# Paged decode attention in one core's kernel: cache pages transposed in 32 by 32 blocks on VectorE, scores in small tiles, pages gathered by GpSimd

## What is computed

```python
c_past = cache_ckv[page_table].reshape(b_s, past_len, KV_RANK)          # 8 x 2048 x 256
kpe_past = cache_kpe[page_table].reshape(b_s, past_len, HEAD_ROPE)      # 8 x 2048 x 32
s = jnp.einsum('bqhr,bkr->bhqk', q_lat, c) + jnp.einsum('bqhe,bke->bhqk', q_pe, kpe)
p = jax.nn.softmax(jnp.concatenate(scores, axis=-1), axis=-1)           # past and own token
term = jnp.einsum('bhqk,bkr->bqhr', p[..., off:off + nk].astype(c.dtype), c)
out = term if out is None else out + term                               # PV over both key sets
o = jnp.einsum('bnhr,rhv->bnhv', o_lat, w_uv).reshape(b_, n, N_HEADS * HEAD_V)
return o @ w_o
```

## Time and profile before

| what | value |
|---|---|
| median of 3 runs | 2010.53 us (2008.69 to 2016.31) |
| profiled execution: span from first to last instruction | 2007.1 us |
| the same against the runs | 1.6 us under the fastest, 3.4 us under the median |
| mean granted TensorE clock | 0.993 of full |
| PE, VectorE, ScalarE, GpSimd busy | 98%, 64%, 41%, 7% |
| decode loop | 1507 to 1585 us of the span |

### The profile page before, as it was taken

How to read it: one execution, slowest core, us unless ns; L and a number is a source line. 1 busy time by engine, 2 the same in 40 slices (tenths; PEclk the granted TensorE clock), 3 DMA queues, 4 the chain that set the end, 5 groups by cost and what they waited for, 6 DMA issues and landing times.

```text
span 2007.1 us, 41612 instructions
## 1 busy us (share of the span) xinstructions
PE 1960.4 (98%) x17604; PEld 1875.2 (93%) x17604; DVE 1277.0 (64%) x1771; ACT 820.4 (41%) x1243; POOL 132.8 (7%) x231
## 2 busy tenths in 40 slices
PE   8999999988999999999999999999989999999999
PEld 7999999987999999999999999997666799999998
DVE  6445486697469577576884856655764349668474
ACT  5332233343245244255452534454654244345252
POOL 3002002010000000000000000000047000000000
PEclk9999999989999999999999999999999999999999
DMA  7233234864342322234322322231248422323222
GB/s 151 84 102 88 75 93 115 269 140 100 95 137 85 120 89 95 77 105 116 97 85 85 127 85 86 84 101 51 54 119 231 149 71 83 127 85 120 91 74 75
DMA packets 260624, 211.55 MB, mean 105 GB/s; under 512 B 42372, under 2 KB 235426, under 8 KB 260450
## 3 DMA queue, kind: packets, MB, share of 16 engines
q1 hardware_dynamic: 248528, 187.52, 31.9%
q0 software_dynamic: 6656, 13.69, 2.4%
q10 hardware_dynamic: 5266, 7.85, 1.2%
HBM read 195.29 MB, written 10.33 MB: 102 GB/s over the span
## 4 chain that ended last, share of the span: by engine, by line
PE 67%; DVE 3%; ACT 2%; issue 2%; SPq 1%; DMA 1%; DVEq 0%; ACTq 0%
PE ps L2459 25%; PE ps L2487 25%; PE ps L2388 6%; PE ps L2401 2%; PE ps L2947 1%; PE ps L3053 1%; PE ps L3209 1%; PE ps L3086 1%; SPq L654 1%; SPq L639 1%; DMA cb<-cache_ckv 1%; PE ps L2841 1%; PE ps L3030 1%; DVE wl L1668 0%; DVE xl L1619 0%
## 5 line engine op out<-in xcount | busy, mean ns | idle before, releaser
L2388 PE MATMUL ps<-xh,wh 128*128 128x260 f32 x1088 | 286.9, 285 | 2.6 <-DVE xl L1619 1.4
L2388 PE MATMUL ps<-xl,wh 128*128 128x260 f32 x1088 | 283.7, 283 | 0.0
L2487 PE MATMUL ps<-xoh,wh 128*128 128x260 f32 x992 | 281.3, 284 | 1.3 <-DVE sq L1835 1.3
L2487 PE MATMUL ps<-xoh,wl 128*128 128x260 f32 x992 | 281.0, 283 | 0.0
L2487 PE MATMUL ps<-xol,wh 128*128 128x260 f32 x992 | 280.6, 283 | 0.0
L2459 PE MATMUL ps<-xh,wh 128*128 128x260 f32 x872 | 228.8, 284 | 0.6 <-DVE wl L1668 0.6
L1067 ACT ACTIVATE wh<-rw 128x1024 fp32r<-128x1024 f32 (+1 forms) x135 | 138.8, 1029 | 218.6 <-PE ps L2459 151.7
L2459 PE MATMUL ps<-xl,wh 128*128 128x260 f32 x872 | 227.0, 282 | 0.0
L2388 PE MATMUL ps<-xh,wl 128*128 128x260 f32 x1088 | 219.3, 283 | 0.0
L990 ACT ACTIVATE wh<-raw 128x1024 fp32r<-128x1024 f32 (+1 forms) x90 | 100.4, 1116 | 283.4 <-PE ps L2388 250.5
L2388 PEld LDWEIGHTS ps<-xh,wh 128*128 128x128 f32 x1088 | 205.6, 189 | 6.9 <-issue 3.9
(11 more groups left out here) (550 smaller groups left out, 4202.2 us busy)
## 6 DMA issues: line engine op xcount, KB each, us to landing
rw<-ffn_w_gate SPq DMA_DIRECT2D x33, 1024.0 KB, 5.4
rw<-ffn_w_up SPq DMA_DIRECT2D x33, 1024.0 KB, 8.0
rw<-ffn_w_down SPq DMA_DIRECT2D x12, 2048.0 KB, 7.8
raw<-ffn_w_gate SPq DMA_DIRECT2D x22, 512.0 KB, 3.9
raw<-ffn_w_up SPq DMA_DIRECT2D x22, 512.0 KB, 3.9
raw<-ffn_w_down SPq DMA_DIRECT2D x16, 704.0 KB, 4.8
rw<-ffn_w_down SPq DMA_DIRECT2D x6, 1536.0 KB, 6.7
cb<-cache_ckv SPq DMA_DIRECT2D x72, 128.0 KB, 3.7
```

Source lines behind the costliest of these rows:

```text
L2388: got = mm(ps[0:width, bank + half, 0:HALF], w[par_][:, k * width:k * width + width], src[:, k0 + k, half * HALF:half * HALF + HALF], star ...
L2487: got = mm(ps[:, bank + mat, T0], w[:, cols], src[:, j, k, :], start=first and k == 0 and m == 0 and s == 0, stop=k == 3 and m == 1, skip_ ...
```

## The change

The pages are no longer transposed on PE.

1. **Gathers.** GpSimd computes, for every partition, the row of the cache to read (`rows_of`; four casts and one multiply-add on the page table, which is now loaded onto all 128 partitions). One indirect DMA then fetches four pages: partition p receives four consecutive positions, 4 KB of latents or 512 B of rotary keys. A sequence needs 4 of each, and all are issued by GpSimd. SyncE issues no pages any more. For b of 2 and later the order is keys of b, then pages of b; the waits are the same (`d_o`).
2. **Block transposes on VectorE.** `turned(b, c)` is one instruction that transposes every 32x32 block in place, from `kb` (128x512) for c = 0 and from a quarter of `cb` (128x1024) for c = 1 to 4. It waits for the arrival (c below 2) and for the scores of b-1 that read the same part.
3. **Scores.** After a block transpose a partition group of 32 holds 32 latent coordinates of a quarter of the positions. `past_scores(b, c)` contracts 32 coordinates at a time in 32x32 tiles: 16 matmuls of 128 columns for each 32 coordinates (four row groups by four column groups), into PSUM banks 0 to 3, 9 such units for each sequence. The queries must then lie on every partition group: they are written to DRAM once and read back replicated (9 DMAs on GpSimd, during the prompt's attention).
4. **Order.** VectorE turns c = 0 and 1 of b+1, takes the maximum of b over four banks, then turns c = 2 to 4 of b+1. PE's order for one b: turn the probabilities of b, all scores of b+1, PV of b. The copy to `pbT` moves to ScalarE, and the copy to `ob` stands one sequence later.
5. **Around it.** `wo_half(0, 0)` moves from the last b into the end of the prompt's attention, some PSUM banks of the output projection change (`WO_BANKS`), and `wide_hi` and `wide_lo` (the last two columns of the projection's weights) stand a little later.

```diff
-        def page_loader(eng, arrived, ckv, kpe):
...
-                for g in ckv:
-                    eng.dma_start(cb[j][:, g, :], inp["cache_ckv"][bass.ds(numbers[b][g], 1)].rearrange("a p r -> p (a r)")).then_inc(arrived[j], 16)
...
+            def gather(src, dst, b, arrived):
+
+                table = inp[src].rearrange("n (u v) r -> (n u) (v r)", v=ROWS)
+                for g in range(NQ):
+                    G.indirect_dma_start(dst[b % 3][:, ROWS * g:ROWS * (g + 1), :].rearrange("p v r -> p (v r)"), None, table,
+                                         bass.IndirectOffsetOnAxis(ap=rows_of[:, NQ * b + g:NQ * b + g + 1], axis=0)).then_inc(arrived[b % 3], 16)
...
+            def keys(b):
+
+                if b >= 3:
+                    pool.wait_ge(d_t, (NCT + 1) * (b - 3) + 1)
+                gather("cache_kpe", kb, b, d_kin)
...
+                elif b == 2:
+                    pool.wait_ge(a_ol, NH // 2)
+                else:
+                    pool.wait_ge(d_o, b - 2)
+                gather("cache_ckv", cb, b, d_in)
...
+            def turned(b, c):
+
+                if c < 2:
+                    dve.wait_ge(d_in[b % 3] if c else d_kin[b % 3], (b // 3 + 1) * 16 * NQ)
                 if b >= 1:
-                    dve.wait_ge(d_s, b)
-                copy(cbT[:, q // 4, (q % 4) * 512:(q % 4) * 512 + 512], ps[:, (0, 1, 7)[(b * 9 + q) % 3], :]).then_inc(d_td, 1)
+                    dve.wait_ge(d_s, (NCT + 1) * (b - 1) + c + 1)
+                if c == 0:
+                    V.transpose(kbT, kb[b % 3].rearrange("p g e -> p (g e)")).then_inc(d_t, 1)
+                else:
+                    V.transpose(cbT[:, c - 1, :, :].rearrange("p q (g u) -> p g q u", u=HP),
+                                cb[b % 3][:, :, 2 * HP * (c - 1):2 * HP * c].rearrange("p g (q r) -> p g q r", q=2)).then_inc(d_t, 1)
...
+            def past_scores(b, c):
+
+                if b == 0 and c == 0:
+                    pe.wait_ge(d_qr, 16 * (1 + 2 * NQ))
+                if b >= 1 and c == 0:
+                    pe.wait_ge(d_e, b)
+                pe.wait_ge(d_t, (NCT + 1) * b + c + 1)
+                for q in range(2 if c else 1):
+                    n = 2 * (c - 1) + q
+                    for a in range(NQ):
+                        rows = slice(HP * a, HP * a + HP)
+                        w, keys_ = (qrep[n // NQ][rows, n % NQ, b, :], cbT[rows, c - 1, q, :]) if c else (qpe[rows, b, :], kbT[rows, :])
+                        for j in range(NQ):
+                            got = mm(ps[HP * j:HP * j + HP, a, 0:P], w, keys_[:, P * j:P * j + P],
+                                     start=c == 0, stop=c == NCT and q == 1, skip_group_check=True)
+                got.then_inc(d_s, 1)
```

More of the change, by code:

```diff
@@ L71 @@
 KB = PAST // NQ
+NCT = R // (2 * HP)
+ROWS = PAGE // HP
 NEG = -1e30
@@ L3196, in _ @@
             weighted(NH // 2 - 1)
-            for q in range(6, 9):
-                turned(0, q)
-            def wo_half(d, half, k0, k1):
-                pe.wait_ge(w_lo, WO0 + d + 1)
-                hi_, lo_ = (wh[(WO0 + d) % 2], wl[(WO0 + d) % 2]) if d < 2 else (w4h[:, d - 2], w4l[:, d - 2])
-                for k in range(k0, k1):
-                    for m, (w, srcs_) in enumerate(((hi_, (xh, xl)), (lo_, (xh,)))):
-                        for s, src in enumerate(srcs_):
-                            got = mm(ps[:, d + 4 * half, 0:HALF], w[:, k * P:k * P + P], src[:, k, half * HALF:half * HALF + HALF],
-                                     start=k == 0 and m == 0 and s == 0, stop=k == KD - 1 and m == 1)
-                if half == 1:
-                    got.then_inc(w_used, 1)
@@ L3237, in _ @@
+            for c in range(3):
+                past_scores(0, c)
+            pe.wait_ge(a_ol, NH // 2)
+            wo_half(0, 0, NH // 2 - 2, KD)
+            for c in range(3, NCT + 1):
+                past_scores(0, c)
+            for b in range(NB):
                 pe.wait_ge(d_e, b + 1)
@@ L3243, in _ @@
                 if b + 1 < NB:
-                    for q in range(4, 9):
-                        turned(b + 1, q)
-                else:
-                    turn(ps[0:NB, 7, 0:P], mb[:, :])
-                    turn(ps[0:NB, 7, P:2 * P], lb[:, :]).then_inc(d_rt, 1)
-                    wo_half(1, 0, 0, 3)
+                    for c in range(NCT + 1):
+                        past_scores(b + 1, c)
+                else:
+                    turn(ps[0:NB, 0, 0:P], mb[:, :])
+                    turn(ps[0:NB, 0, P:2 * P], lb[:, :]).then_inc(d_rt, 1)
+                    wo_half(1, 0, 0, 4)
                 pe.wait_ge(d_pe, b + 1)
@@ L3461, in _ @@
             G.memset(qlat[:, :, :, :], 0.0)
[L3462 to L3466 removed]
+            pool.wait_ge(q_c, QT)
+            G.memset(qpe[:, :, :], 0.0).then_inc(m_zero, 1)
+            pool.wait_ge(m_zero, 1)
+            pool.wait_ge(d_pt, 16)
+            for a in range(NQ):
+                own(G.tensor_copy(page_of[HP * a:HP * a + HP, :], pt[HP * a:HP * a + HP, a:NB * NPG:NQ]))
@@ new lines, in _ @@
+            pool.wait_ge(l_qe, 1)
+            pool.dma_start(dr_q, qlat[:, :, :, :].rearrange("p r b h -> p r (b h)")).then_inc(d_qr, 16)
+            pool.wait_ge(d_qr, 16)
+            for a in range(NQ):
+                for r in range(RT):
+                    pool.dma_start(qrep[r][HP * a:HP * a + HP].rearrange("p s b h -> p s (b h)"),
+                                   dr_q.rearrange("(s p) r n -> r p s n", s=NQ)[r]).then_inc(d_qr, 16)
+            for b in range(NB):
+                if b < 2:
+                    pages(b)
+                    keys(b)
+                else:
+                    keys(b)
+                    pages(b)
```

242 lines of the change are left out of this document (82 added, 160 removed).

## The result

The changed kernel takes 2077.53 us (median of 4 runs, 2075.30 to 2080.28); the kernel before, beside it on the same chip, took 2009.61 (4 runs, 2008.28 to 2016.31). The ratio is 1.0336, 95% interval 1.0318 to 1.0354: some 68 us slower, outside the forecast's range (1994 to 2027) and far from its 2004.

A forecast was written before the change was run, and what follows sets the result against it. The prediction took PE to bound the decode loop, with pages close behind. Loop and tail gains summed to -10.7 us at full clock, -2.5 at half; the middle, -6.6 from 2010.5, gave 2004, range 1994 to 2027.

The forecast's parts named there:

- What bounds the kernel before: Decode loop: PE-bound, busy 9.0 to 9.5 of 10 us, pages close behind, DMA engines at 0.90 and 0.93.
- VectorE's term: Per sequence: block transposes 1.22 us each, 0.69 for the key's; 6.4 us of work in all.
- rival in which VectorE becomes the bound: Decode loop: at 2.44 us a transpose VectorE works 11.8 us a sequence; +14, 2024; chance 0.09.
- GpSimd's term: Page loads: 8 gathers a sequence, all issued by GpSimd, 1.0 us each, ends 0.54 and 2.76.
- rival on GpSimd: Gather issues become the bound above 1.43 us: 2020 at 1.65, 2069 at 2.76; chance 0.19.
- rule on shared ports: VectorE in two-port mode makes descriptors of GpSimd's DMAs wait; each gather issue then between 1.0 and 2.2 us.
- PE's term: Scores: 288 records at 8 ns, 2.3 us a sequence; PE's work falls to 4.9 us, page transposes gone.
- 25 ns between starts: Score matmuls: the skill's closest spacing of starts; by it nothing to gain, 2010. PE staying the bound: chance 0.08.
- The chain: Decode loop: 8.17 us from pages landing through PV, then 9.35 for next pages; 8.76 a sequence against 9.67.
- the two waits: Added: VectorE's maximum of b waits for pages b+1; GpSimd's pages b+2 wait for PV of b-1.
- The clock: PE half idle, so half clock part of the time; at half clock throughout 8.2 us lost, -2.5; middle -6.6.
- Transfers bind: Decode loop: at 253 GB/s a sequence's 2.36 MB take 9.3 us; -3.5, 2007; chance 0.10.

The follow-up runs named there:

- key_blocks_only: Kernel before with VectorE block transposes for the rotary keys alone, no gathers, no small tiles; 2009.92 us, ratio 0.9993.
- gathers_in_ffn: Kernel before plus 16 idle back-to-back gathers on GpSimd in the last feed-forward stage; 2019.92 us, ratio 1.0047.
- gathers_alone: Kernel before with its page loads replaced by the change's eight gathers per sequence, PE still transposing; 2066.56 us, ratio 1.0274.
- tiles_page_rows: Changed kernel with the plain page transfers of the kernel before, one cache row per partition, in place of gathers; 2037.13 us, ratio 1.0130.
- tiles_kept_warm: tiles_page_rows with each maximum before the page wait, PV between halves of the next latent scores, three idle matmuls per sequence; 2037.02 us.
- tiles_alone: Changed kernel with gathers replaced by one plain transfer per page into the gathers' layout (32 partitions, same pieces); 2050.83 us, ratio 1.0197.

## Why the prediction was wrong

- **What bounds the kernel before**: right. PE, with the transfers close behind; in key_blocks_only the waits for pages take 2.7 us more.
- **VectorE's term**: right, 1.22 and 0.71 us. The rival in which VectorE becomes the bound did not occur.
- **GpSimd's term**: the issue was sized nearly right (0.956 us, 1.26 from start to start with 0.30 between), so eight take 9.8 us and not 8.0. The rival on GpSimd was priced by its own queue, with a threshold of 1.43 us; below that it was to cost nothing. This is the step that failed first: while the gathers run, word of PE's work reaches the other engines late (9.7 us in gathers_in_ffn, 3.5 to 7.5 in gathers_alone), and PE stands. It is worth 42 us on top of the tiles, 55 alone. The chain was drawn as if every wait ended when the work before it ended, and under gathers it doesn't. The rule on shared ports that the prediction cited from the Trainium skill, "SBUF — State Buffer", section "SBUF: two separate sides", was not it: the gathers' issues stayed at 0.956 us beside the transposes.
- **PE's term**: wrong in size and in kind. The 8 ns a record was a sixteenth of a full record's 123, and what spoke for it were records with 8 columns; 128 records with 128 columns took 1.9 to 2.0 us at full clock (15 to 16 ns) and 3.03 at half clock (24). At these paces the scores of a sequence take 4.3 to 6.8 us without stops, not 2.3 (and PE's work was 4.8 us by the prediction's own terms, not 4.9). The nearest row in columns was the 64x64 one, 31 ns. And nobody counted the instructions: 288 records with their weight loads are 576, some 640 with the rest, two and a half refills of 256 per sequence, with a stop at about every other one. The prediction counted GpSimd's issues and VectorE's operations, but took PE's instructions as free. (The 25 ns between starts of the Trainium skill, "TensorE: Matmul & The Clock Gate", section "Wait — 56ns, not 53.3ns?", does not hold for these tiles either: 15 to 16 ns.)
- **The chain**: its form was right, pages of b+2 behind PV of b-1 behind all scores of b, with gaps that alternate. Without gathers, in tiles_page_rows, its length was 17.4 us to PV's end, not 8.17: PE turns the probabilities before it starts the scores, so exp and turn (0.9 and 1.1) are in it; the key's transpose adds 0.7; the scores take 8.9 with their stop and not 4.2 beside the transposes; PV takes 3.9 (granted clock 0.61 from 1548 to 1552), not 1.93. Undoing the two waits gave only 5 of 26 us back; PE's part does not get shorter by it.
- **The clock**: expected at half "part of the time". In the windows above it was 0.56 to 0.75. PV took 17.6/6 = 2.9 us a sequence in place of 1.93 (the row of L3180 above), 8 us over eight sequences, as much as the sum had for scores and PV together at the worst (8.2). tiles_kept_warm got some of the clock back and gained nothing, but its idle matmuls also cost time.
- **Transfers bind**: not in the change (pages were waited for 4.1 us). That they are the next limit is hinted at by key_blocks_only, not shown.

## What to carry to other kernels

Count the instructions that a change gives to each engine, weight loads too, and compare their number per microsecond with a stretch where that engine runs without "issue" stops: here 24 records a microsecond (weight loads and matmuls, 1467 from 1520 to 1580) went through without a stop of that kind, and the 45 of tiles_page_rows (2710 in the same 60 us) did not. Look at what a new kind of instruction does to the engines that it shares nothing with in the program; an idle copy of it in a quiet stage costs one run and would have shown that gathers hold PE up, though not how much it costs in the loop. When a profile gives "issue" or "remote" for a wait, follow the program: here the engine that stood was waiting for one that had not heard of its own last work. Where gathers are needed, pauses after every four cost nothing in the feed-forward; in the loop four at a time still delayed each maximum by 2 to 4 us.

## What was not expected of the hardware

- While indirect gathers run back to back on GpSimd, what PE has finished reaches the other engines late, 2 to 8 us in the loop and 9.7 in the feed-forward, where 0.01 is usual: 9.11 us of standstill of PE during 16 gathers, 3.4 around 8, none during 40 plain transfers, none with a pause after every four.
- PE's instructions come in blocks of 256 (16384 bytes, 0.9 to 1.5 us each once moving); with 45 records a microsecond PE reaches the end of a block and stands there for 1 to 5 us, even with no page transfer on the queues.
- Plain transfers into 32 partitions with pieces of 4 KB moved less at full DMA share than those into 128 partitions with 1 KB, in one window of each. That of tiles_alone, columns as in the earlier trace rows:

```profile
1547.00:1551.00 4.00, 4.00 (x165) 2.96 (x163) 2.04 (x2) 0.60 (x1) 3.35 (x7) 0.52 1.04 217
```

  217 GB/s at a DMA share of 1.04, where the kernel before moves 317 at 1.01.
